# An expert's biases by one product per bank, and nine rows of the context chain spread over the partitions by products with a row of ones

## The reference

```python
# first block: for each of 32 experts e, on the tokens that chose it
gt = xb @ w_gate[e] + b_gate[e]
up = xb @ w_up[e] + b_up[e]
gt = jnp.minimum(gt, SWIGLU_LIMIT)
up = jnp.clip(up, -SWIGLU_LIMIT, SWIGLU_LIMIT)
hdn = gt * jax.nn.sigmoid(SWIGLU_ALPHA * gt) * (up + 1.0)
return hdn @ w_down[e] + b_down[e]

# second block, layer 0, context stream (rows of 1024 numbers act on all tokens)
h   = ctx * (1.0 + s1c) + sh1c
mix = chunk_mlp(h, ...)          # gelu(h @ w_in), layer norm with a_norm_g, a_norm_b, spatial gate, @ w_out
ctx = layer_norm_2(DN_ALPHA * ctx + g1c * mix, ln_g, ln_b)
ffn_ctx = peer_ffn(ctx * (1.0 + s2c) + sh2c, ...)
```

## Time and profile before

| | |
|---|---|
| time, median of 3 runs | 3594.15 us (3589.74 to 3594.68) |
| profiled execution, first to last instruction | 3592.4 us |
| PE busy | 3214.3 us (89%) |
| DVE busy | 1769.1 us (49%) |
| ACT busy | 1092.2 us (30%) |
| moved | 1379.94 MB, mean 384 GB/s |
| the experts' stage | about 375 to 1370 us |

### The profile page before, as it was taken

One profiled execution on the slowest core, in us unless ns is written; L12 is line 12 of the kernel. 1 busy time (PEld: TensorE's weight loads), 2 busy tenths in 40 slices (PEclk: granted clock), 3 DMA queues, 4 the chain that ended last, 5 costly groups with the idle time before them and its releaser, 6 DMA issues. The chain is left out here.

```text
span 3592.4 us, 34407 instructions
## 1 busy us (share of the span) xinstructions
PE 3214.3 (89%) x11268; PEld 1432.4 (40%) x11268; DVE 1769.1 (49%) x4114; ACT 1092.2 (30%) x2961; POOL 863.9 (24%) x796
## 2 busy tenths in 40 slices
PE   8999999999999996989888778998888988887776
PEld 6575433433334432433344223333334444422222
DVE  0153111211130126676775677668764477667664
ACT  1231111111111113433343344545333224434333
POOL 0000000000000002434344444444441024444442
PEclk9999899999999998999999999999999999999999
DMA  9915899999999999999999999999998069999997
GB/s 406 394 71 227 354 428 426 423 418 425 411 428 427 398 427 414 415 422 420 422 407 406 421 420 421 409 415 420 413 416 339 30 268 400 421 421 418 418 421 325
DMA packets 158245, 1379.94 MB, mean 384 GB/s; under 512 B 18601, under 2 KB 19113, under 8 KB 26610
## 3 DMA queue, kind: packets, MB, share of 16 engines
q0 software_dynamic: 111360, 805.46, 54.3%
q1 hardware_dynamic: 46706, 572.24, 38.1%
HBM read 1376.48 MB, written 1.15 MB: 383 GB/s over the span
## 5 line engine op out<-in xcount | busy, mean ns | idle before, releaser
L2935 PE MATMUL ps<-sb_arena,sb_diag 128*128 128x512 f32 x3072 | 1494.3, 625 | 314.4 <-ACT sb_diag L2910 303.7
L1783 POOL DMA_INDIRECT sb_arena<-in_uv,sb_idx x768 | 851.2, 1108 | 2349.7 <-PE ps L2935 1101.7
L2865 DVE SCALAR_TENSOR_TENSOR sb_arena<-sb_arena,sb_H 128x1024 f32<-128x1024 f32 x768 | 941.0, 1226 | 600.6 <-DMA sb_arena<-in_uv,sb_idx 403.7
L2935 PEld LDWEIGHTS ps<-sb_arena,sb_diag 128*128 128x128 f32 x3072 | 563.8, 195 | 1194.5 <-ACT sb_diag L2910 642.4
L1446 PE MATMUL ps<-sb_ring,sb_arena 128*64 128x512 f32 x3072 | 676.9, 596 | 3.9 <-DMA sb_ring<-in_moe 3.9
L2901 ACT ACTIVATE sb_act<-sb_dots 128x1 f32<-128x1 f32 x768 | 155.0, 202 | 1082.9 <-DVE sb_arena L2865 1077.7
L1446 PEld LDWEIGHTS ps<-sb_ring,sb_arena 128*64 128x64 f32 x3072 | 215.0, 137 | 444.6 <-issue 432.8
L2910 ACT ACTIVATE sb_diag<-sb_consts,sb_act 128x128 f32<-128x128 f32 x768 | 308.4, 402 | 29.6 <-PE ps L2935 4.4
L1646 DVE TENSOR_SCALAR sb_arena<-ps 128x512 f32<-128x512 f32 x32 | 22.1, 692 | 594.6 <-PE ps L1446 579.0
L2905 ACT ACTIVATE sb_act<-sb_act,sb_wts 128x1 f32<-128x1 f32 x768 | 226.2, 295 | 24.9
L180 PE MATMUL ps<-sb_ring,sb_arena 128*128 128x512 f32 x416 | 182.0, 594 | 1.9 <-DVE sb_arena L755 1.3
(11 more groups left out here) (358 smaller groups left out, 2442.5 us busy)
## 6 DMA issues: line engine op xcount, KB each, us to landing
sb_ring<-in_moe SPq DMA_DIRECT2D x192, 2048.0 KB, 16.3
sb_ring<-in_w_mod SPq DMA_DIRECT2D x24, 2048.0 KB, 19.2
sb_ring<-in_w_in SPq DMA_DIRECT2D x10, 2048.0 KB, 23.5
sb_ring<-in_a_w_in SPq DMA_DIRECT2D x8, 2048.0 KB, 16.4
sb_ring<-in_b_w_in SPq DMA_DIRECT2D x8, 2048.0 KB, 11.9
sb_ring<-in_w_q SPq DMA_DIRECT2D x6, 2048.0 KB, 13.8
sb_arena<-in_uv,sb_idx POOLq DMA_INDIRECT x768, 15.2
sb_ring<-in_a_w_out SPq DMA_DIRECT2D x4, 2048.0 KB, 13.6
```

What stands on the lines that cost most here:

```text
L1783: pool.indirect_dma_start(row_buffer(m, n), None, d[f"uv{layer}"], bass.IndirectOffsetOnAxis(m.idx[:, pair % 2, k:k + 1], 0))\
L2865: nc.vector.scalar_tensor_tensor(out=u, in0=u, scalar=1.0, in1=m.H[:, order[i], :], op0=ALU.mult, op1=ALU.mult, accum_out=m.dots[:, n_ % P ...
L2935: last = nc.tensor.matmul(out[h], m.diag[n_ % DIAGS], uv[b][:, D + h * 512:D + (h + 1) * 512], start=opens, stop=ends)
```

## The change

The biases: `biases` now has 128 partitions of 512 columns (gate's left half, gate's right half, up's left, up's right, 32 partitions each; four transfers instead of two). `select` is 64 rows by 2 x 64 columns, per bank, made by one multiplication on all 128 partitions. Two products, of 64 rows and 128 columns each, fill the two banks. A constant `half` of two columns is new.

The rows: each of the nine rows now comes as two pieces of 2 KB, to partitions 0 and 32 of its place. PE multiplies each piece with a row of ones (one row by 128 columns) into banks 7 and 5, and ACT copies both banks over the row's place. The nine rows come in four sets, at experts 0 (2 rows), 4 (2), 6 (3) and 14 (2), and DVE waits for ACT's count of rows.

```diff
@@ constants
+        "half": j // NE % 2 == np.arange(2)[None, :],
@@ new
+def row_halves(sp, M, home, src, name):
+    sp.dma_start(home[0:64:32, 0:512], src.rearrange("o (n c) -> (o n) c", n=2)).then_inc(M(name), 16)
@@ Context
-            sp.dma_start(dst, mod_row(d, 0, 1, which).to_broadcast([P, D])).then_inc(M("context_in"), 16)
+            row_halves(sp, M, dst, mod_row(d, 0, 1, which), "context_h_in")
...
-                sp.dma_start(dst, src.to_broadcast([P, D])).then_inc(M("context_end_in"), 16)
+                row_halves(sp, M, dst, src, "context_mod_in")
@@ Context.tensor
+        def spread(kind, e):
+            pe.wait_ge(M(f"context_{kind}_in"), 16 * len(self.sets[kind]))
+            for i in self.sets[kind]:
+                both = [plan["row", i, n] for n in range(2)]
+                for where in both:
+                    open_bank(where, e)
+                for n, where in enumerate(both):
+                    rows_ = slice(32 * n, 32 * n + 1)
+                    banks.fill(nc.tensor.matmul(m.ps[:, where[0], :], m.const("ones")[rows_, :], self.homes[i][rows_, 0:512],
+                                                start=True, stop=True), where)
+        yield 0
+        spread("h", 0)
...
+            if n:
+                yield (4, 6)[n - 1]
+                spread(("norm", "end")[n - 1], (4, 6)[n - 1])
...
+        yield 14
+        spread("mod", 14)
@@ Context.scalar
+        def spread_out(kind):
+            for i in self.sets[kind]:
+                both = [plan["row", i, n] for n in range(2)]
+                for where in both:
+                    banks.wait_full(act, where)
+                for n, where in enumerate(both):
+                    banks.free_chained(act, nc.scalar.activation(self.homes[i][:, n * 512:(n + 1) * 512], m.ps[:, where[0], :], ACT.Copy), where)
+                act.sem_inc(M("context_rows"), 1)
@@ moe, expert
-                for n in range(2):
-                    for which in range(2):
-                        rows = slice(which * NE, (which + 1) * NE)
-                        nc.tensor.matmul(m.ps[n * SLOTS:(n + 1) * SLOTS, 4 + which, :], x.select[rows, :],
-                                         x.biases[rows, n * 512:(n + 1) * 512], start=True, stop=False, skip_group_check=True)
+                for which in range(2):
+                    rows = slice(which * 2 * NE, (which + 1) * 2 * NE)
+                    nc.tensor.matmul(m.ps[:, 4 + which, :], x.select[rows, :, :].rearrange("p n c -> p (n c)"), x.biases[rows, :],
+                                     start=True, stop=False, skip_group_check=True)
@@ moe, select
-                nc.vector.tensor_copy(x.select[0:2 * NE, :], m.const("expert")[0:2 * NE, bass.ds(e, 1)].to_broadcast([2 * NE, SLOTS]))\
-                    .then_inc(M(name("select_ready", p)), 1)
+                nc.vector.tensor_scalar(x.select, m.const("half").rearrange("p (n c) -> p n c", c=1).to_broadcast([P, 2, SLOTS]),
+                                        m.const("expert")[:, bass.ds(e, 1)], None, ALU.mult).then_inc(M(name("select_ready", p)), 1)
```

More of the change, by code:

```diff
@@ L871, in __init__, with spread @@
         self.groups = [(t, p, i) for t in range(TT) for i in range(2) for p in range(2)]
-        names = [("turn", t, n) for t in range(TT) for n in range(2)]
-        names += [("z", n, t) for n in range(3) for t in range(TT)] + [("mixed", t, n) for t in range(TT) for n in range(2)]
-        names += [("z", 3, t) for t in range(TT)] + [("turned", t, n) for t in range(TT) for n in range(2)]
+        self.homes = self.h_mods + self.norm_rows + [self.ends[0], self.ends[1], self.mods[1]] + [self.ends[2], self.mods[0]]
+        self.sets = {"h": range(0, 2), "norm": range(2, 4), "end": range(4, 7), "mod": range(7, 9)}
+        def spread(kind):
+            return [("row", i, n) for i in self.sets[kind] for n in range(2)]
+        names = spread("h") + [("turn", t, n) for t in range(TT) for n in range(2)]
+        names += [("z", 0, t) for t in range(TT)] + spread("norm") + [("z", 1, t) for t in range(TT)] + spread("end")
+        names += [("z", 2, t) for t in range(TT)] + [("mixed", t, n) for t in range(TT) for n in range(2)]
+        names += [("z", 3, t) for t in range(TT)] + [("turned", t, n) for t in range(TT) for n in range(2)] + spread("mod")
         names += [("sum", n, t) for n in range(2) for t in range(TT)] + [("back", t, n) for t in range(TT) for n in range(2)]
@@ L1021, in gelu @@
             ring.done(act, f"context{n}")
+        def spread_out(kind):
[6 more added lines that the diff above has]
+                act.sem_inc(M("context_rows"), 1)
+        yield 0
+        spread_out("h")
         for t in range(TT):
@@ L1027, in scalar @@
         gelu(0)
+        yield 4
+        spread_out("norm")
         yield 5
         gelu(1)
+        yield 6
+        spread_out("end")
         for t in range(TT):
@@ L1039, in scalar @@
             turned("turned", t)
+        yield 14
+        spread_out("mod")
         yield 18
@@ L1106, in vector @@
         yield 0
-        dve.wait_ge(M("context_in"), 32)
+        dve.wait_ge(M("context_rows"), 2)
         for t in range(TT):
@@ L1114, in vector @@
         yield 7
-        dve.wait_ge(M("context_norm_in"), 48)
+        dve.wait_ge(M("context_bias_in"), 16)
+        dve.wait_ge(M("context_rows"), 4)
         values_end(0)
@@ L1134, in vector @@
             yield e
-            dve.wait_ge(M("context_end_in"), 80)
+            dve.wait_ge(M("context_rows"), 9)
             cols = slice(n * 512, (n + 1) * 512)
@@ L1175, in __init__ @@
         self.total = m.part(5056, NE + 2)
-        self.biases = m.part(5120, D)
+        self.biases = m.part(5120, 512)
         self.b_down = m.part(7168, D)
@@ L1189, in __init__ @@
         self.ye = m.part(2560, 512)
-        self.select = m.part(3072, SLOTS)
+        self.select = m.part(3072, 2, SLOTS)
 class Router:
@@ L1208, in rest @@
         d, x, M = self.d, self.x, self.M
-        for dst, src in ((x.biases[0:NE, :], d["b_gate"]), (x.biases[NE:2 * NE, :], d["b_up"]), (x.b_down[0:NE, :], d["b_down"])):
-            sp.dma_start(dst, src).then_inc(M("biases_in"), 16)
+        for which, name in enumerate(("b_gate", "b_up")):
+            for n in range(2):
+                at = (2 * which + n) * NE
+                sp.dma_start(x.biases[at:at + NE, :], d[name][:, n * 512:(n + 1) * 512]).then_inc(M("biases_in"), 16)
+        sp.dma_start(x.b_down[0:NE, :], d["b_down"]).then_inc(M("biases_in"), 16)
     def loaded(self, sp):
-        sp.wait_ge(self.M("biases_in"), 3 * 16)
+        sp.wait_ge(self.M("biases_in"), 5 * 16)
         sp.wait_ge(self.M("ctx_in"), 16)
```

6 lines of the change are left out of this document (3 added, 3 removed).

## The result

The changed kernel takes 3623.32 us (median of 4 runs, 3621.07 to 3626.57), the kernel before 3591.94 on the same chip; the ratio is 1.0089, interval 1.0075 to 1.0102. It is 31 us slower. Taken as a difference, 18.8 us were forecast and 31.4 measured: 12.6 too few.

The account below looks back on a forecast made before the run. PE's work up to 945.9 us was taken as the path: first rows 4.2, further rows 12.7, expert 14 1.0, biases 0.8, transfers 0, sum +18.7 on the span of 3592.4; forecast 3613, range 3601 to 3620.

Parts of the forecast that it names:

- PE's work up to 945.9 is the path: Experts' stage: whatever PE gains or loses before 945.9 us, the end gains or loses; 18.7 us on PE's path.
- Saved transfers are worth 0: Nine row transfers of 512 KB removed before 945.9 bring 0 us, bounds 0 and -8.7, as PE waits for nothing there.
- Rival 1: Transfers bind throughout the stage: PE's 18.7 us fall into slack, 8.7 us are saved, 3585.5; chance 4%.
- Rival 2: PE's delay is absorbed later, by waits for chunks after 1193 and in the next stage: some 3600; chance 5%.
- rivals 3: Further rows in a set cost only 1.06 to 1.31 us, ACT's copies being hidden: 3606; chance 6%.
- 5: Packing doesn't happen, small products on PE run in sequence: 25 us more, 3638; chance 2%.
- Biases 1.06 us instead of 1.02: Two bias products per expert take two steps on PE, 0.04 us more than four side by side; 20 experts, +0.8 us.
- A first row 1.06 us: First row of each set finds its banks free and costs PE 1.06 us; four make 4.2 us.
- A further row 2.53 us: Each further row in a set waits for ACT's copies of the row before: 2.53 us, five make 12.7 us.
- Expert 14 behind the turns, +1.0: In expert 14 the first row waits for ACT's copies of eight turns filling banks 7 and 5: +1.0 us.
- The clock holds in the sets: PE's granted clock stays up in experts 0, 4, 6 and 14; a fall there would show the forecast wrong.
- rival 4: The clock falls as PE works and idles in turn, 5 us behind each of four sets, 20 in all: 3633; chance 4%.

Follow-up runs that it names:

- five single rows: The change with h's two rows brought by transfer and the other seven each spread in an expert of its own: 3598.03 against 3590.16, ratio 1.0022.
- the version without falls: The change with 64 rows of weights, all zero but the first, plus a 128-row filling product before each further row: 3611.07 against 3590.39, ratio 1.0054.
- both profiles: The changed kernel profiled twice; the second time it took 3623.99 against 3590.39 for the kernel before, ratio 1.0089.
- The wide products: The change with each spreading product made of 64 rows of ones and 64 rows of tokens, same waits: 3612.60 against 3591.30, ratio 1.0059.
- the thin and the full filling: The change with a useless product before each further row, of one row (3623.28, ratio 1.0088) or 128 rows (3616.46, ratio 1.0072), against 3591.30.
- the selected rows: The change with the same values, but 64 rows of weights per spreading product, all zero but the first: 3613.23 against 3590.39, ratio 1.0067.

## Why the prediction was right and wrong

- *PE's work up to 945.9 is the path, and all lost before it reaches the end.* Right: +27.4 at expert 17, +27.8 at expert 31, +26.8 on the span.
- *Saved transfers are worth 0, bounds 0 and -8.7.* Right: 3590.01 against 3590.16 without them. Rival 1 fell, and with it the reading of a share of 1.00 as a limit. Rival 2 fell too (27.4 at expert 17, 27.8 at expert 31), as did rivals 3 (the step was 2.74) and 5 (a row's two products ran side by side).
- *Biases 1.06 us instead of 1.02, +0.8 in all.* Right, 1.06 in two kernels; over 16 experts 0.66 us by the starts in the trace, where 0.64 follows from it.
- *A first row 1.06 us.* Right: five single rows and 16 bias groups are 5.95 us by the trace, 5.94 by the terms.
- *A further row 2.53 us.* Mis-sized by a little: 2.74 (597.00 to 599.74). I took the handovers from the nearest rows as 0.04 and 0.05; here they are 0.13 from PE's end to ACT (598.13 to 598.26) and 0.25 from ACT's end to PE (599.49 to 599.74), while ACT's pair is 1.23 and not 1.31. Five rows: 1.1 us.
- *Expert 14 behind the turns, +1.0.* About right: PE waits 1.2 us for ACT's copies there. With these the sum is 19.9 and not 18.7; the version without falls measured 20.7 by the medians, and over experts 1 to 16 its trace shows 15.97 us where the terms give 15.98.
- *The clock holds in the sets* was **the step that failed**: rival 4, which I gave 4% and priced at 20. It happened in all four sets, in both profiles. In the first its cost in experts 4, 6 and 14 was 1.7 + 4.2 + 3.1 = 9.0 us, and about 1.7 in expert 0; in the second 10.0 in the three; between the change and the version without falls lie 12.9 us in the medians of one set of runs. I had dismissed it because waits of 1.2 us for chunks left the clock at 1.00. But those waits stand between products of all 128 rows, and the set's products have one row; the set's waits are also longer, 1.6 us, and up to two follow each other closely. I compared the idle time and not what stood around it. I also priced a fall by the 11 us of 372 to 383, where it cost 1.7 to 4.2 here. And that stretch was read too simply: PE had waited 2.0 and 2.3 us before 358.77, but from there to 365.88 it was busy without a gap, on products of 32 rows, and the granted clock stayed at 0.50 all the time:

```profile
358.77 7.18 PE L1405 MATMUL ps<-sb_arena 32*128 32x512 f32 x8 [2.31 <-PEq L386]
...
359.00:366.00 7.00, 7.00 (x9) 2.37 (x9) 1.46 (x7) 0.00 (x0) 1.26 (x3) 0.50 1.02 430
```

All thirteen profiles show the same, with the clock rising only behind it, between 372 and 382 us, where PE's products have 128 or 64 rows or lie side by side. That doesn't prove the part of the rows, as the clock might have needed longer in any case, but it was a hint in the trace of before that busy time and clock can part.

The Trainium skill, TensorE: Matmul & The Clock Gate, section on depth-cycling of the PSUM queue, tells of a kernel on bf16 data whose frequent small idle times between groups of matmuls make the clock swing. Taken as a rule, that made rival 4 the forecast, and the trace agrees with it (0.74 to 0.92 in the four windows). The wide products, with the same idle times, agree in one set of four only. What the section doesn't say, the thin and the full filling show: of two kernels whose PE is busy equally long, one keeps its clock in two sets (4 and 6) in which the other loses it.

The advice of the Trainium skill, TensorEngine Tiling (Array Packing), section PSUM Bottleneck, to share the copies between ScalarE and VectorE, holds as far as it goes: the step fell from 2.74 to 2.22 us.

What stays open is how the two parts add up: wide products with the waits let it fall once in four sets, filled waits between thin products in two of four, both changed in none, a thin row alone in none of seven. What decides whether a given set falls was not found, and apart from the change itself each version has a single profile. Nor was it tried to spread h's two rows apart from each other.

## What to carry to other kernels

A stage can show transfers at full share and PE at full busy time at once; look for the moments at which the queue of transfers is empty, for they tell which of the two is the path, and take a kernel without the transfers to confirm it. Products in small tiles that already run side by side don't get cheaper by being merged: count steps, not instructions. And be wary of thin products with waits between them in a stream of full ones. Here they kept the clock when set down one at a time, or with more rows (zeros did) and a filled wait together; more rows alone, or a filled wait alone, kept it in three and in two sets of four. Where the queue of transfers runs ahead of PE, a transfer that repeats the row costs nothing, as here.

## What the runs showed that I had not expected

- Four sets of two or three rows (8 to 12 hardware matmuls) drew the granted clock to 0.50, its lower level of 1.2 GHz, for a stretch that outlasted the set, and cost more by that (11 to 13 us) than the idle time in them (5 x 1.7 us).
- A product over 64 rows of weights of which 63 are zero kept the clock about as well as one of 64 ones: 22.8 and 21.3 us above before, against 31 to 34 for one row.
- A useless product of 128 rows in a wait made the kernel faster: 25.2 us above before, where a thin one in its place gave 32.0, and 20.7 instead of 22.8 together with the selected rows (the latter two not told apart by their intervals).
- The experts' stage begins at a lower clock whose end moves from run to run: with no set on PE, expert 0 took 30.3 us in the profile of before, 28.8 in that of the biases alone and 26.9 in that of the kernel without row transfers. Single profiles of these kernels differ by 3 us through that alone.
